# Six of ten PSUM banks kept across the down stage, and the acts-times-gates product moved from VectorE to GpSimd

## The chip, the cores and the metric

The kernel runs on one core of one Trainium2 chip. The metric is the device time of one execution in microseconds (us), the median of three runs. Engines are named as in the profile: PE is TensorE, DVE is VectorE, ACT is ScalarE, POOL is GpSimd, SP is SyncE, which here only issues transfers.

## The reference

One trunk layer on 1024 tokens of width 1024: a gated recurrence and an attention, then PEER, a retrieval over 128 x 128 = 16384 single-neuron experts, and a last norm. The change touches only the second half of PEER:

```
experts = (e1 * PEER_NKEYS + e2).reshape(t, hk)      # 128 experts per token
gates = jax.nn.softmax(top_s, axis=-1).reshape(t, hk)
pre = einsum('td,tkd->tk', xb, u_tab[eb])            # "up"
act = gelu(pre) * gb
y   = einsum('tk,tkd->td', act, v_tab[eb])           # "down"
```

All is float32.

## The kernel before

**Two ways to the same sum.** The first three tiles of 128 tokens (F = 3) are computed by rows: each token's 128 expert rows are fetched by number and added with a weight. The other five tiles (640 tokens) are computed densely: the activation of every expert is multiplied by a gate, zero where the expert wasn't picked, and the down stage multiplies this 640 x 16384 matrix by the whole table v. Both ways run side by side in `experts_down` (L1562), which is the stage of this case.

**The dense way.** The 128 keys x go in NG = 32 groups of C = 4. For each key, SP loads a piece of v (512 KB, ring of 3), the activations (320 KB, ring of 4, the tile `acts_times_gates`), and for each group the gates (1280 KB). `multiply(x)` (L1650) puts acts times gates in place. To multiply float32 on TensorE, every operand is split in a rounded high part and the rest: ACT writes `v_hi` (L1642) and, once the product is there, `w_hi` (L1644). DVE writes the rests: `low_of_v(x)` (L1666, tile `v_lo`) and `low(x)` (L1658, tile `w_lo`). TensorE then makes, for a group, BANKS = 10 sums (five token tiles, two halves of 512 columns): j = 0 to 9, each of 4 keys x 3 products = 12 matmuls. A sum lands in one of the 8 PSUM banks in turn, and DVE adds it to `y` (`add(n, j)`, L1672), which frees the bank. TensorE's group n+1 may start only when all four `low` and `low_of_v` of that group are done (L1714, L1715). The four parts are double buffered by group.

**The row way.** GpSimd issues `fetch(k)` (L1616), an indirect transfer of one row per partition (512 KB) into a ring of 5, and DVE adds it with its weight (`add_row(k)`, L1680). There are 3 x 128 = 384. Fetch k waits until row k-5 has been added (L1619).

**The order on DVE** is written out by hand (L1698 to L1709). Group n has ten steps j. In step j DVE runs, if they are due, multiply and low_of_v of a key of the next group (j = 0, 2, 5, 7) or low of that key (j = 1, 3, 6, 8), then the rows whose turn it is (364 rows over 320 steps, so 11.375 a group), and then `add(n, j)`. The order on GpSimd (L1623 to L1631) sets how many fetches are issued before the transfer queue goes on to the next key:

```
asked = lambda x: min(max(FIRST_ROWS + ROW_RING + (x - C) * (AXPYS - FIRST_ROWS) // NK, FIRST_ROWS), AXPYS)
```

that is, 25 + floor((x - 4) * 2.84375) fetches come ahead of key x.

Of the kernel before, what the change touches and what calls it, by code (L numbers as in the profile page):

```python
# [4 lines left out]
ALU = mybir.AluOpType  # L5
ACT = mybir.ActivationFunctionType
AX_X = mybir.AxisListType.X
F32 = mybir.dt.float32
# [4 lines left out]
P = 128  # L13
HALF = 512
# [1173 lines left out]
def experts_up(nc, d, m, sem):  # L1188
# [15 lines left out]
    DOTS = F * P  # L1204
    RING = 6
    QUARTERS = 4 * NK
# [27 lines left out]
    with ExitStack() as own_memory:  # L1234
# [14 lines left out]
        gate_hi, gate_lo = sb("gateT_hi", [P, 2, P], F32R), sb("gateT_lo", [P, 2, P])  # L1249
        rows = sb("u_rows", [P, RING, D])  # L1250
        dots = m.row_weight
# [14 lines left out]
        key_step, route_turned, routeT_done = sem("key_step"), sem("route_turned"), sem("routeT_done")  # L1266
        rows_known, fetched = sem("rows_known"), [sem(f"u_row_in{b}") for b in range(RING)]
        dot_done, dots_read, weighted = sem("dot_done"), sem("dots_read"), sem("row_weights_done")
# [12 lines left out]
        with nc.Block() as block:  # L1281
# [127 lines left out]
            def _(pool):  # L1409
# [7 lines left out]
                def fetch(k):  # L1417
                    f, slot = divmod(k, P)
                    if slot == 0:
                        pool.wait_ge(rows_known, f + 1)  # L1420
                    if k >= RING:
                        pool.wait_ge(dot_done, k - RING + 1)
                    pool.indirect_dma_start(rows[:, k % RING], None, d.peer_u, bass.IndirectOffsetOnAxis(  # L1423
                        ap=m.row_of[:, f, slot:slot + 1], axis=0)).then_inc(fetched[k % RING], 16)
# [137 lines left out]
def experts_down(nc, d, m, sem):  # L1562
# [5 lines left out]
    NT, F = S // P, m.ROWS_TILES  # L1568
    DENSE = S - F * P
    C, PART = 4, 32  # L1570
    NG = NK // C
    BANKS = (NT - F) * D // HALF
    RING = 8
    V_RING, W_RING, ROW_RING = 3, 4, 5
    AXPYS = F * P
    FIRST_ROWS = 20
# [1 line left out]
    with ExitStack() as own_memory:  # L1578
        sb = lambda n, s, t=F32: own_memory.enter_context(nc.sbuf_tensor(n, s, t))
        prod = sb("acts_times_gates", [P, W_RING, DENSE])  # L1580
        gate = sb("gates_group", [P, 2, DENSE // PART, C, PART])
# [1 line left out]
        whi, wlo = sb("w_hi", [P, 2, C, DENSE], F32R), sb("w_lo", [P, 2, C, DENSE], F32R)  # L1583
        vhi, vlo = sb("v_hi", [P, 2, C, D], F32R), sb("v_lo", [P, 2, C, D], F32R)
        rows = sb("v_rows", [P, ROW_RING, D])
        out = own_memory.enter_context(nc.psum_tensor("expert_out", [P, RING, HALF], F32))

        y_in, y_rest_in = sem("x2_in"), sem("x2_rest_in")
        a_in = [sem(f"acts_in{b}") for b in range(W_RING)]
        g_in = [sem(f"gates_in{b}") for b in range(2)]  # L1590
        v_in = [sem(f"v_in{b}") for b in range(V_RING)]
        prod_done, whi_done, wlo_done = sem("prod_done"), sem("w_hi_done"), sem("w_lo_done")
        vhi_done, vlo_done = sem("v_hi_done"), sem("v_lo_done")
        out_done, out_read = sem("expert_out_done"), sem("expert_out_read")
        fetched, row_added = [sem(f"v_row_in{b}") for b in range(ROW_RING)], sem("v_row_added")

        with nc.Block() as block:
            @block.sync
# [15 lines left out]
            @block.gpsimd  # L1614
            def _(pool):
                def fetch(k):  # L1616
                    slot, f = divmod(k, F)
                    if k >= ROW_RING:
                        pool.wait_ge(row_added, k - ROW_RING + 1)  # L1619
                    pool.indirect_dma_start(rows[:, k % ROW_RING], None, d.peer_v, bass.IndirectOffsetOnAxis(  # L1620
                        ap=m.row_of[:, f, slot:slot + 1], axis=0)).then_inc(fetched[k % ROW_RING], 16)

                asked = lambda x: min(max(FIRST_ROWS + ROW_RING + (x - C) * (AXPYS - FIRST_ROWS) // NK, FIRST_ROWS), AXPYS)  # L1623
                for k in range(asked(0)):
                    fetch(k)
                for x in range(NK):
                    pool.wait_ge(vhi_done, x + 1)
                    for k in range(asked(x), asked(x + 1)):
                        fetch(k)
                for k in range(asked(NK), AXPYS):  # L1630
                    fetch(k)  # L1631
# [14 lines left out]
            @block.vector  # L1646
            def _(dve):
                v = nc.vector

                def multiply(x):  # L1650
                    n, c = divmod(x, C)
                    dve.wait_ge(a_in[x % W_RING], 16 * (x // W_RING + 1))
                    if c == 0:
                        dve.wait_ge(g_in[n % 2], 16 * (n // 2 + 1))
                    tokens = prod[:, x % W_RING].rearrange("p (t k) -> p t k", k=PART)
                    v.tensor_tensor(tokens, tokens, gate[:, n % 2, :, c, :], ALU.mult).then_inc(prod_done, 1)  # L1656

                def low(x):  # L1658
                    n, c = divmod(x, C)
                    dve.wait_ge(whi_done, x + 1)  # L1660
                    if c == 0 and n >= 2:
                        dve.wait_ge(out_done, BANKS * (n - 1))
                    v.tensor_tensor(wlo[:, n % 2, c], prod[:, x % W_RING], whi[:, n % 2, c].bitcast(F32), ALU.subtract  # L1663
                                    ).then_inc(wlo_done, 1)

                def low_of_v(x):  # L1666
                    n, c = divmod(x, C)
                    dve.wait_ge(vhi_done, x + 1)
                    v.tensor_tensor(vlo[:, n % 2, c], vt[:, x % V_RING], vhi[:, n % 2, c].bitcast(F32), ALU.subtract
                                    ).then_inc(vlo_done, 1)  # L1670

                def add(n, j):  # L1672
                    t, half = divmod(j, 2)
                    bank = BANKS * n + j
                    dve.wait_ge(out_done, bank + 1)
                    cols = slice(half * HALF, (half + 1) * HALF)
                    v.tensor_tensor(m.y[:, F + t, cols], m.y[:, F + t, cols], out[:, bank % RING], ALU.add  # L1677
                                    ).then_inc(out_read, 1)

                def add_row(k):  # L1680
                    slot, f = divmod(k, F)
                    dve.wait_ge(fetched[k % ROW_RING], 16 * (k // ROW_RING + 1))
                    if k >= F:
                        dve.wait_ge(row_added, k - F + 1)
                    v.scalar_tensor_tensor(out=m.y[:, f], in0=rows[:, k % ROW_RING],  # L1685
                                           scalar=m.row_weight[:, f, slot:slot + 1], in1=m.y[:, f],
                                           op0=ALU.mult, op1=ALU.add).then_inc(row_added, 1)

                dve.wait_ge(y_in, 16)
                for k in range(FIRST_ROWS):  # L1690
                    add_row(k)
                for x in range(C):
                    low_of_v(x)
                    multiply(x)
                    low(x)
                dve.wait_ge(y_rest_in, 16)
                added = lambda s: FIRST_ROWS + s * (AXPYS - FIRST_ROWS) // (NG * BANKS)
                for n in range(NG):  # L1698
                    for j in range(BANKS):
                        for x in range(C):  # L1700
                            if n + 1 < NG and j == x * BANKS // C:
                                multiply(C * (n + 1) + x)
                            if n + 1 < NG and j == x * BANKS // C + 1:
                                low(C * (n + 1) + x)
                            if n + 1 < NG and j == x * BANKS // C + (0 if BANKS < 3 * C else 2):
                                low_of_v(C * (n + 1) + x)
                        for k in range(added(BANKS * n + j), added(BANKS * n + j + 1)):
                            add_row(k)
                        add(n, j)  # L1709

            @block.tensor
            def _(pe):
                for n in range(NG):
                    pe.wait_ge(wlo_done, C * (n + 1))  # L1714
                    pe.wait_ge(vlo_done, C * (n + 1))  # L1715
                    for j in range(BANKS):
                        t, half = divmod(j, 2)
                        bank = BANKS * n + j
                        tokens, cols = slice(t * P, (t + 1) * P), slice(half * HALF, (half + 1) * HALF)
                        if bank >= RING:  # L1720
                            pe.wait_ge(out_read, bank - RING + 1)
                        terms = [(a, e, c) for c in range(C) for a, e in ((whi, vhi), (whi, vlo), (wlo, vhi))]
                        for k, (a, e, c) in enumerate(terms):
                            last = nc.tensor.matmul(out[:, bank % RING], a[:, n % 2, c, tokens], e[:, n % 2, c, cols],  # L1724
                                                    start=k == 0, stop=k == len(terms) - 1)
                        last.then_inc(out_done, 1)


# [185 lines left out]
```

## Time and profile before

| | |
|---|---|
| median of 3 runs | 3281.61 us (3280.7 to 3283.81) |
| profiled execution | 3266.46 us, span 3264.7 us |
| DVE, PE, POOL, ACT busy | 2415.6, 2913.1, 1339.1, 1211.5 us |
| down stage, first row added to last sum added | 2220.16 to 3240.61 us |
| one group of it | 30.75 us |

Busy time over the whole span mixes several stages; the argument needs only the down stage, so the rows below are read with a window. A DVE row's duration overlaps the next one's start by some 0.08 us; what an instruction costs in a full queue is the distance between two starts.

### The profile page before, as it was taken

The page shows a single profiled execution, that of the slowest core. Times are in us where ns is not written, and L with a number is a line of the kernel's source. Part 1 is how long each engine was busy: PE and PEld are TensorE (multiplying, and loading weights), DVE is VectorE, ACT ScalarE, POOL GpSimd, SP SyncE. Part 2 cuts the span into 40 slices and gives each one's busy share as a digit, 9 for nine tenths or more (in the row PEclk, how much of TensorE's full clock was granted, in tenths as well). Part 3 has the DMA queues.
Part 4 walks back from the last instruction along what each step waited for, and adds up shares of the span by engine and source line. Part 5 has one row for each costly group of instructions (what it writes and reads, how often), then busy time and mean ns, then how long its engine had stood idle before and what let it go on. Part 6 is the DMA issues. An engine that isn't in the chain of part 4 may idle for free. (4 is left out here: it accounts for less than half of the span.)

```text
span 3264.7 us, 40188 instructions
## 1 busy us (share of the span) xinstructions
PE 2913.1 (89%) x15015; PEld 2398.5 (73%) x15015; DVE 2415.6 (74%) x4285; ACT 1211.5 (37%) x2462; POOL 1339.1 (41%) x1095
## 2 busy tenths in 40 slices
PE   7998998988798889999999999991999999999996
PEld 3345545543798888999999999991777777777775
DVE  1073353622397699979788988875999999999997
ACT  2112223211111225777778778751222222222221
POOL 1030000000287457555545555543444464454455
PEclk9988899899899999999999999995999999999998
DMA  5000001011210248998989999988999999999996
GB/s 152 1 20 20 0 1 52 0 58 45 65 34 27 93 163 298 335 352 321 351 324 375 345 325 357 357 333 327 360 356 351 361 348 355 355 350 344 356 357 219
DMA packets 309203, 754.28 MB, mean 231 GB/s; under 512 B 22848, under 2 KB 133440, under 8 KB 306448
## 3 DMA queue, kind: packets, MB, share of 16 engines
q0 software_dynamic: 111104, 403.02, 33.7%
q1 hardware_dynamic: 196848, 344.50, 30.0%
q10 hardware_dynamic: 1056, 4.19, 0.3%
q8 instruction: 119, 1.95, 0.2%
q14 instruction: 76, 0.62, 0.1%
HBM read 659.35 MB, written 92.27 MB: 230 GB/s over the span
## 5 line engine op out<-in xcount | busy, mean ns | idle before, releaser
L1620 POOL DMA_INDIRECT v_rows<-in_peer_v,row_numbers x384 | 523.9, 1364 | 524.3 <-DVE y L1685 432.5
L1325 PE MATMUL expert_pre<-h2T,uT_hi 128*128 128x320 f32 x4096 | 679.8, 315 | 58.7 <-DVE uT_lo L1510 31.7
L1423 POOL DMA_INDIRECT u_rows<-in_peer_u,row_numbers x384 | 539.5, 1405 | 434.6 <-DVE row_weights L1527 377.7
L1325 PEld LDWEIGHTS expert_pre<-h2T,uT_hi 128*128 128x128 f32 x4096 | 621.5, 192 | 64.0 <-DVE uT_lo L1510 35.3
L1724 PE MATMUL expert_out<-v_hi,w_hi 128*128 128x512 f32 x1280 | 510.5, 399 | 133.5 <-DVE w_lo L1663 133.5
L1685 DVE SCALAR_TENSOR_TENSOR y<-v_rows,row_weights,y 128x1024 f32<-128x1024 f32 x384 | 487.0, 1277 | 40.9 <-DMA v_rows<-in_peer_v,row_numbers 23.9
L1724 PE MATMUL expert_out<-v_lo,w_hi 128*128 128x512 f32 x1280 | 506.1, 395 | 0.0
L1724 PE MATMUL expert_out<-v_hi,w_lo 128*128 128x512 f32 x1280 | 505.9, 395 | 0.0
L1527 DVE CUSTOM_DVE_ANT_0 u_rows<-u_rows,h_rows_kept 128x1024 f32<-128x1024 f32 x384 | 469.2, 1249 | 5.3 <-DMA u_rows<-in_peer_u,row_numbers 5.3
L1724 PEld LDWEIGHTS expert_out<-v_hi,w_hi 128*128 128x128 f32 x1280 | 245.5, 192 | 197.1 <-DVE w_lo L1663 146.0
L1644 ACT ACTIVATE w_hi<-acts_times_gates 128x640 fp32r<-128x640 f32 x128 | 94.8, 741 | 735.6 <-DVE acts_times_gates L1656 610.3
L1325 PE MATMUL expert_pre<-h2T,uT_lo 128*128 128x320 f32 x2048 | 343.0, 308 | 0.0
L1325 PEld LDWEIGHTS expert_pre<-h2T,uT_lo 128*128 128x128 f32 x2048 | 312.7, 188 | 0.0
L1724 PEld LDWEIGHTS expert_out<-v_hi,w_lo 128*128 128x128 f32 x1280 | 244.8, 191 | 52.3
L1724 PEld LDWEIGHTS expert_out<-v_lo,w_hi 128*128 128x128 f32 x1280 | 245.6, 192 | 50.9
L1510 DVE TENSOR_TENSOR uT_lo<-u_chunk,uT_hi 128x1024 fp32r<-128x1024 f32 x104 | 127.2, 1223 | 139.0 <-ACT uT_hi L1361 129.2
L1383 ACT ACTIVATE second_hot_lo<-second_hot_hi,gateT_lo 128x128 fp32r<-128x128 f32 x640 | 203.2, 392 | 64.3 <-DVE second_hot_hi L1521 62.0
L1677 DVE TENSOR_TENSOR y<-y,expert_out 128x512 f32<-128x512 f32 x320 | 217.1, 678 | 2.6 <-PE expert_out L1724 2.4
L1386 ACT ACTIVATE second_hot_hi<-second_hot_hi,gateT_hi 128x128 fp32r<-128x128 f32 x640 | 203.5, 392 | 0.0
L1368 ACT ACTIVATE pick_memory<-spread_ps 128x512 f32<-128x512 f32 x160 | 179.6, 1122 | 21.4 <-PE spread_ps L1317 19.5
L1092 POOL CAST wq_hi<-wq_tile 128x1024 fp32r<-128x1024 f32 x16 | 16.6, 1039 | 407.0 <-DMA wq_tile<-in_peer_wq 360.6
L1375 ACT ACTIVATE expert_acts<-expert_pre 128x320 f32<-128x320 f32 x256 | 112.4, 440 | 185.4 <-PE expert_pre L1325 183.7
(264 smaller groups left out, 4324.5 us busy)
## 6 DMA issues: line engine op xcount, KB each, us to landing
u_chunk<-in_peer_u_turned SPq DMA_DIRECT2D x128, 512.0 KB
v_chunk<-in_peer_v SPq DMA_DIRECT2D x128, 512.0 KB
acts_dram<-expert_acts SPq DMA_DIRECT2D x128, 320.0 KB
gates_dram<-pick_memory SPq DMA_DIRECT2D x20, 2048.0 KB
acts_times_gates<-acts_dram SPq DMA_DIRECT2D x128, 320.0 KB
gates_group<-gates_dram SPq DMA_DIRECT2D x32, 1280.0 KB
wq_tile<-in_peer_wq SPq DMA_DIRECT2D x16, 512.0 KB, 3.9
w_qkv<-in_w_in SPq DMA_DIRECT2D x12, 512.0 KB, 7.1
```

Of the source, the lines that this page charges most:

```text
L1325: last = nc.tensor.matmul(pre[:, (2 * c + half) % 4, 0:WIDTH], part[:, c % 2, k], m.h2T[:, t, k, HALVES[half]], start=n == 0, stop=n == le ...
L1368: A(spread[:, part % 2, :, col * GROUP:(col + 1) * GROUP].rearrange("p e t -> p t e"), spread_ps[:, g % 2], ACT.Copy).then_inc(spread_read, 1)
L1375: A(act_out[:, c % 2, half * WIDTH:(half + 1) * WIDTH], pre[:, (2 * c + half) % 4, 0:WIDTH], ACT.Gelu_apprx_tanh).then_inc(act_done, 1)
L1383: A(second_lo[:, g % SLOTS, j], second_hi[:, g % SLOTS, j].bitcast(F32), ACT.Identity, scale=gate_lo[:, t % 2, first + j:first + j + 1])
L1386: last = A(second_hi[:, g % SLOTS, j], second_hi[:, g % SLOTS, j].bitcast(F32), ACT.Identity, scale=gate_hi[:, t % 2, first + j:first + j ...
L1423: pool.indirect_dma_start(rows[:, k % RING], None, d.peer_u, bass.IndirectOffsetOnAxis(ap=m.row_of[:, f, slot:slot + 1], axis=0)).then_inc ...
L1510: v.tensor_tensor(ulo[:, c % 2], u[:, c % 2], uhi[:, c % 2].bitcast(F32), ALU.subtract).then_inc(ulo_dve, 1)
L1527: v.tensor_tensor_reduce(out=rows[:, k % RING], in0=rows[:, k % RING], in1=m.h2_kept[:, f], scale=1.0, scalar=0.0, op0=ALU.mult, op1=ALU.a ...
L1620: pool.indirect_dma_start(rows[:, k % ROW_RING], None, d.peer_v, bass.IndirectOffsetOnAxis(ap=m.row_of[:, f, slot:slot + 1], axis=0)).then ...
L1677: v.tensor_tensor(m.y[:, F + t, cols], m.y[:, F + t, cols], out[:, bank % RING], ALU.add).then_inc(out_read, 1)
L1685: v.scalar_tensor_tensor(out=m.y[:, f], in0=rows[:, k % ROW_RING], scalar=m.row_weight[:, f, slot:slot + 1], in1=m.y[:, f], op0=ALU.mult, ...
L1724: last = nc.tensor.matmul(out[:, bank % RING], a[:, n % 2, c, tokens], e[:, n % 2, c, cols], start=k == 0, stop=k == len(terms) - 1)
```

## The change

Six of the ten sums (j = 1, 2, 4, 6, 7, 9) get a PSUM bank for themselves and are accumulated in it over all 32 groups; DVE adds them to `y` once, in the last group. The other four (`TURNING`: 0, 3, 5, 8) share the two banks that are left and are added in every group, as before. `multiply` leaves DVE and stands in GpSimd's program, ahead of the fetches of the same key. Everything else, the order of low, low_of_v and the rows among it, stays where it was.

```
-    RING = 8
+    TURNING = [0, 3, 5, 8]
+    KEPT = [j for j in range(BANKS) if j not in TURNING]
+    RING = 8 - len(KEPT)
...
+        def place(n, j):
+            if j in KEPT:
+                i = KEPT.index(j)
+                return i // 2, i % 2, i
+            i = TURNING.index(j)
+            return (len(KEPT) + i) // 2, i % 2, len(KEPT) + (len(TURNING) * n + i) % RING
...
+                def multiply(x):
+                    n, c = divmod(x, C)
+                    pool.wait_ge(a_in[x % W_RING], 16 * (x // W_RING + 1))
+                    if c == 0:
+                        pool.wait_ge(g_in[n % 2], 16 * (n // 2 + 1))
+                    tokens = prod[:, x % W_RING].rearrange("p (t k) -> p t k", k=PART)
+                    pool.tensor_tensor(tokens, tokens, gate[:, n % 2, :, c, :], ALU.mult).then_inc(prod_done, 1)
...
                 for x in range(NK):
+                    multiply(x)
                     pool.wait_ge(vhi_done, x + 1)
                     for k in range(asked(x), asked(x + 1)):
                         fetch(k)
...
                 for x in range(C):
                     low_of_v(x)
-                    multiply(x)
                     low(x)
...
-                            if n + 1 < NG and j == x * BANKS // C:
-                                multiply(C * (n + 1) + x)
...
-                        add(n, j)
+                        if j in TURNING or n == NG - 1:
+                            add(n, j)
...
-                        if bank >= RING:
-                            pe.wait_ge(out_read, bank - RING + 1)
+                        turn = len(TURNING) * n + TURNING.index(j) if j in TURNING else 0
+                        if turn >= RING:
+                            pe.wait_ge(out_read, turn - RING + 1)
+                        opens = j in TURNING or n == 0
+                        closes = j in TURNING or n == NG - 1
...
-                                                    start=k == 0, stop=k == len(terms) - 1)
+                                                    start=opens and k == 0, stop=closes and k == len(terms) - 1)
```

DVE's queue before, in one half of a group of the down stage (steps 0 to 3, or 5 to 8, which read alike). `acts_times_gates` is written by multiply, `v_lo` by low_of_v, `w_lo` by low; `y` from `v_rows` is a row, `y` from `expert_out` is an add.

```order
L1656 TENSOR_TENSOR acts_times_gates<-acts_times_gates,gates_group 128x640
L1669 TENSOR_TENSOR v_lo<-v_chunk,v_hi 128x1024
L1685 SCALAR_TENSOR_TENSOR y<-v_rows,row_weights,y 128x1024
L1677 TENSOR_TENSOR y<-y,expert_out 128x512
L1663 TENSOR_TENSOR w_lo<-acts_times_gates,w_hi 128x640
L1685 SCALAR_TENSOR_TENSOR y<-v_rows,row_weights,y 128x1024
L1677 TENSOR_TENSOR y<-y,expert_out 128x512
L1656 TENSOR_TENSOR acts_times_gates<-acts_times_gates,gates_group 128x640
L1669 TENSOR_TENSOR v_lo<-v_chunk,v_hi 128x1024
L1685 SCALAR_TENSOR_TENSOR y<-v_rows,row_weights,y 128x1024
L1677 TENSOR_TENSOR y<-y,expert_out 128x512
L1663 TENSOR_TENSOR w_lo<-acts_times_gates,w_hi 128x640
```

The same steps on DVE in the changed kernel, up to the end of step 8 (or 3):

```order
L1680 TENSOR_TENSOR v_lo<-v_chunk,v_hi 128x1024
L1695 SCALAR_TENSOR_TENSOR y<-v_rows,row_weights,y 128x1024
L1687 TENSOR_TENSOR y<-y,expert_out 128x512
L1674 TENSOR_TENSOR w_lo<-acts_times_gates,w_hi 128x640
L1695 SCALAR_TENSOR_TENSOR y<-v_rows,row_weights,y 128x1024
L1680 TENSOR_TENSOR v_lo<-v_chunk,v_hi 128x1024
L1695 SCALAR_TENSOR_TENSOR y<-v_rows,row_weights,y 128x1024
L1674 TENSOR_TENSOR w_lo<-acts_times_gates,w_hi 128x640
L1695 SCALAR_TENSOR_TENSOR y<-v_rows,row_weights,y 128x1024
L1687 TENSOR_TENSOR y<-y,expert_out 128x512
```

The multiplies are gone, and the adds of the kept banks with them; low stands at the same step, now behind fewer instructions.

GpSimd's queue in the down stage before is 384 fetches with nothing between them. In the changed kernel it reads, with the semaphores that each instruction waits for (`v_row_added` counts the rows that DVE has added, `acts_in` and `gates_in` are landed transfers):

```order
L1639 TENSOR_TENSOR acts_times_gates<-acts_times_gates,gates_group 128x640 [waits acts_in2]
L1630 DMA v_rows<-in_peer_v,row_numbers 128x1024 [waits v_row_added,v_hi_done]
L1630 DMA v_rows<-in_peer_v,row_numbers 128x1024 [waits v_row_added] x2
L1639 TENSOR_TENSOR acts_times_gates<-acts_times_gates,gates_group 128x640 [waits acts_in3]
L1630 DMA v_rows<-in_peer_v,row_numbers 128x1024 [waits v_row_added,v_hi_done]
L1630 DMA v_rows<-in_peer_v,row_numbers 128x1024 [waits v_row_added] x2
```

Each multiply now stands behind two or three fetches, and the engine takes its queue in order.

## Rows read from the trace of the kernel before

**Rows 1.** Busy time per engine in the steady part of the down stage.
```profile
core 0: us, PE busy (x) PEld busy (x) DVE busy (x) ACT busy (x) POOL busy (x), PEclk, DMA share, GB/s
2300.00:3200.00 900.00, 838.71 (x3581) 683.17 (x3580) 891.77 (x992) 203.04 (x237) 464.14 (x337) 0.98 0.99 352
```

**Rows 2.** Waits, same stretch: who, for whom, total us, times, longest us.
```profile
POOL v_rows L1620 <- DVE y L1685: 393.8, 240, 4.7
...
PE expert_out L1724 <- DVE w_lo L1663: 61.3, 28, 4.3
...
DVE y L1685 <- DMA v_rows<-in_peer_v,row_numbers: 7.3, 5, 2.6
```

**Rows 3.** Groups of instructions, DVE, 2220 to 3241 us: busy, mean ns, idle before.
```profile
L1685 DVE SCALAR_TENSOR_TENSOR y<-v_rows,row_weights,y 128x1024 f32<-128x1024 f32 x384 | 487.0, 1277 | 40.9 <-DMA v_rows<-in_peer_v,row_numbers 23.9 <-DMA y<-x_dram 16.8
L1677 DVE TENSOR_TENSOR y<-y,expert_out 128x512 f32<-128x512 f32 x320 | 217.1, 678 | 2.6 <-PE expert_out L1724 2.4
...
L1663 DVE TENSOR_TENSOR w_lo<-acts_times_gates,w_hi 128x640 fp32r<-128x640 f32 x128 | 104.5, 816 | 3.2 <-ACT w_hi L1644 3.2
L1656 DVE TENSOR_TENSOR acts_times_gates<-acts_times_gates,gates_group 128x640 f32<-128x640 f32 x128 | 104.5, 816 | 1.8 <-DMA gates_group<-gates_dram 1.8
```

**Rows 4.** Timeline of DVE within one group: start, duration, instruction.
```profile
2598.52 0.82 DVE L1656 TENSOR_TENSOR acts_times_gates<-acts_times_gates,gates_group 128x640 f32<-128x640 f32 x1
2599.26 1.22 DVE L1669 TENSOR_TENSOR v_lo<-v_chunk,v_hi 128x1024 fp32r<-128x1024 f32 x1
2600.39 1.28 DVE L1685 SCALAR_TENSOR_TENSOR y<-v_rows,row_weights,y 128x1024 f32<-128x1024 f32 x1
2601.59 0.68 DVE L1677 TENSOR_TENSOR y<-y,expert_out 128x512 f32<-128x512 f32 x1
2602.18 0.82 DVE L1663 TENSOR_TENSOR w_lo<-acts_times_gates,w_hi 128x640 fp32r<-128x640 f32 x1
2602.92 1.28 DVE L1685 SCALAR_TENSOR_TENSOR y<-v_rows,row_weights,y 128x1024 f32<-128x1024 f32 x1
...
2608.44 1.22 DVE L1669 TENSOR_TENSOR v_lo<-v_chunk,v_hi 128x1024 fp32r<-128x1024 f32 x1
```

**Rows 5.** Timeline of POOL beside them, and one fetch later on.
```profile
2601.94 0.94 POOL L1620 DMA_INDIRECT v_rows<-in_peer_v,row_numbers  x1 [2.73 <-DVE y L1685]
...
2608.36 2.12 POOL L1620 DMA_INDIRECT v_rows<-in_peer_v,row_numbers  x1 [0.30 <-issue]
...
2659.43 3.37 POOL L1620 DMA_INDIRECT v_rows<-in_peer_v,row_numbers  x1 [0.31 <-issue]
```

**Rows 6.** Timeline of ACT beside them.
```profile
2608.55 0.74 ACT L1644 ACTIVATE w_hi<-acts_times_gates 128x640 fp32r<-128x640 f32 x1 [6.47 <-DVE acts_times_gates L1656]
```

**Rows 7.** Timeline of PE at the ends of two groups.
```profile
3178.95 0.39 PE L1724 MATMUL expert_out<-v_hi,w_lo 128*128 128x512 f32 x1
3181.36 0.50 PE L1724 MATMUL expert_out<-v_hi,w_hi 128*128 128x512 f32 x1 [2.02 <-DVE w_lo L1663]
...
3208.48 0.39 PE L1724 MATMUL expert_out<-v_hi,w_lo 128*128 128x512 f32 x1
3212.11 0.50 PE L1724 MATMUL expert_out<-v_hi,w_hi 128*128 128x512 f32 x1 [3.25 <-DVE w_lo L1663]
```

**Rows 8.** GpSimd's float32 tensor_tensor elsewhere: count, min/median/max ns of each.
```profile
L1414 POOL TENSOR_TENSOR uT_lo<-u_chunk,uT_hi x24: 2352/2408/3958, 1085.5 to 1277.2; 128x1024 fp32r<-128x1024 f32 x24
...
L1003 POOL TENSOR_TENSOR decode<-decode x6: 456/461/463, 923.4 to 1117.3; 128x128 f32<-128x128 f32 x6
```

**Rows 9.** Timeline, DVE and POOL, where both ran a two-input instruction.
```profile
1181.64 2.28 DVE L1474 TENSOR_TENSOR pick_memory<-pair_digits,iota 128x2048 f32<-128x2048 bf16 x1
...
1183.96 4.37 DVE L1479 TENSOR_TENSOR pick_memory<-pick_memory,top_indices_f 128x2048 f32<-128x2048 f32 x1
...
1182.50 3.68 POOL L1414 TENSOR_TENSOR uT_lo<-u_chunk,uT_hi 128x1024 fp32r<-128x1024 f32 x1 [4.64 <-ACT uT_hi L1361]
...
1201.00 2.29 DVE L1479 TENSOR_TENSOR pick_memory<-pick_memory,top_indices_f 128x2048 f32<-128x2048 f32 x1
```

More of the change, by code:

```diff
@@ L1585, in experts_down @@
         rows = sb("v_rows", [P, ROW_RING, D])
-        out = own_memory.enter_context(nc.psum_tensor("expert_out", [P, RING, HALF], F32))
+        out = own_memory.enter_context(nc.psum_tensor("expert_out", [P, 8, HALF], F32))
         y_in, y_rest_in = sem("x2_in"), sem("x2_rest_in")
@@ L1593, in experts_down @@
         vhi_done, vlo_done = sem("v_hi_done"), sem("v_lo_done")
-        out_done, out_read = sem("expert_out_done"), sem("expert_out_read")
+        out_done, out_read, kept_read = sem("expert_out_done"), sem("expert_out_read"), sem("kept_out_read")
         fetched, row_added = [sem(f"v_row_in{b}") for b in range(ROW_RING)], sem("v_row_added")
+        def place(n, j):
[4 more added lines that the diff above has]
+            return (len(KEPT) + i) // 2, i % 2, len(KEPT) + (len(TURNING) * n + i) % RING
         with nc.Block() as block:
@@ L1648, in _ @@
                 v = nc.vector
[L1650 to L1656, printed above, removed]
                 def low(x):
@@ L1672, in add @@
                 def add(n, j):
-                    t, half = divmod(j, 2)
-                    bank = BANKS * n + j
-                    dve.wait_ge(out_done, bank + 1)
+                    t, half, bank = place(n, j)
+                    dve.wait_ge(out_done, BANKS * n + j + 1)
                     cols = slice(half * HALF, (half + 1) * HALF)
-                    v.tensor_tensor(m.y[:, F + t, cols], m.y[:, F + t, cols], out[:, bank % RING], ALU.add
-                                    ).then_inc(out_read, 1)
+                    v.tensor_tensor(m.y[:, F + t, cols], m.y[:, F + t, cols], out[:, bank], ALU.add
+                                    ).then_inc(out_read if j in TURNING else kept_read, 1)
                 def add_row(k):
@@ L1716, in _ @@
                     for j in range(BANKS):
-                        t, half = divmod(j, 2)
-                        bank = BANKS * n + j
+                        t, half, bank = place(n, j)
                         tokens, cols = slice(t * P, (t + 1) * P), slice(half * HALF, (half + 1) * HALF)
-                        if bank >= RING:
-                            pe.wait_ge(out_read, bank - RING + 1)
+                        turn = len(TURNING) * n + TURNING.index(j) if j in TURNING else 0
[3 more added lines that the diff above has]
+                        closes = j in TURNING or n == NG - 1
                         terms = [(a, e, c) for c in range(C) for a, e in ((whi, vhi), (whi, vlo), (wlo, vhi))]
                         for k, (a, e, c) in enumerate(terms):
-                            last = nc.tensor.matmul(out[:, bank % RING], a[:, n % 2, c, tokens], e[:, n % 2, c, cols],
-                                                    start=k == 0, stop=k == len(terms) - 1)
+                            last = nc.tensor.matmul(out[:, bank], a[:, n % 2, c, tokens], e[:, n % 2, c, cols],
+                                                    start=opens and k == 0, stop=closes and k == len(terms) - 1)
                         last.then_inc(out_done, 1)
```

## The prediction

> **What bounds the kernel now.** First I read the busy times of the steady part of the down stage [rows 1]. Of 900 us DVE is busy 892, PE 839, and the DMA engines have a share of 0.99; three things are close to their end together, and DVE is the closest. Then the waits [rows 2]: PE waited 61.3 us in 28 pieces, all of them for DVE's `w_lo`, the last thing a group needs before it may start. DVE waited 7.3 us for rows and for nothing else of size. GpSimd waited 393.8 us for DVE's row adds: it is idle, but it is idle because each of its fetches has to wait for a row. Last, the timelines. A group of 120 matmuls starts at 3181.36 and the next at 3212.11, so a group takes 30.75 us; its own matmuls run from 3181.36 to 3208.48 plus one step, 27.2 us [rows 7]. So PE could go 3.5 us a group faster, if DVE let it.
>
> DVE's prices are the distances between two starts [rows 4]: multiply 0.74 us, low_of_v 1.13, a row 1.20, an add 0.60, low 0.74. A group on DVE is 11.375 rows, 10 adds and 4 of each of the others: 13.65 + 6.0 + 10.44 = 30.1 us, against 30.75 measured.
>
> **What the change removes.** All 128 multiplies [rows 3] at 0.74 us: 95 us. The adds of six banks in 31 of 32 groups, 186 of 320, at 0.60 us: 112 us. Together 206 us of DVE's queue, 6.6 us a group, which leaves DVE 23.5 us of work for each group, less than PE's 27.2. A reader who stops here forecasts a gain that ends at PE.
>
> **What it adds: a wait in a circle.** GpSimd's multiply(x) stands behind all fetches before it, and with f = floor((x-4) x 2.84375) the last of these is the (25+f)th, which by the ring of five may start only when DVE has added its (20+f)th row. Call that the releasing row. Written out from L1697 to L1709, DVE comes to exactly this row just ahead of its own low(x), and low(x) needs the product. So for each key DVE adds the releasing row, GpSimd then fetches, then multiplies, ACT then writes `w_hi`, and only then can DVE go on with low(x). No buffer softens this: the ring of five rows is what ties the fetch to the row. Before, the product came from DVE itself, a step ahead.
>
> What DVE has to do between the releasing row and low(x) I counted from the code for x = 4 to 127: (A) low_of_v, row, add, 53 times; (A2) the same with two rows, 8 times; (B) low_of_v, row, 28 times; (C) nothing, 27 times; (D) one row, 7 times. One more, x = 4, has a long list and no stall.
>
> The chain, with time 0 where DVE's next instruction would start:
> - The fetch starts 0.35 us later (2601.94 against 2601.59) and takes 0.94 us when DVE is in an add [rows 4, 5]; I take the same when DVE is idle. It ends at 1.29.
> - When DVE is in low_of_v, the fetch waits for it: the one at 2608.36 ends at 2610.48, which is 0.82 us after low_of_v's end at 2609.66 [rows 4, 5]. So in A, A2 and B it ends at 1.22 + 0.82 = 2.04, in D at 1.28 + 0.82 = 2.10.
> - The multiply of 128x640 on GpSimd is not in the trace. Its float32 tensor_tensor takes 2.41 us for 1024 elements and 0.46 for 128 [rows 8], so 2.18 ns an element more, and 0.46 + 512 x 0.00218 = 1.57 us, if runs of 32 elements cost nothing extra. Lower end: 1.2 us, half of 2.41; in proportion to the elements it would be 1.5, and no row shows GpSimd faster than that. Upper end: the 2.41 us of 1024 elements.
> - ACT's `w_hi` starts 0.03 us after the product and takes 0.74 (2608.55; DVE's multiply before it began 0.74 us before low_of_v at 2608.44 and so ended at 2608.52) [rows 4, 6]; 0.02 more to low.
>
> So in C low starts at 1.29 + 1.57 + 0.79 = 3.65, a stall of 3.65 us. In D: 2.10 + 1.57 + 0.79 - 1.20 = 3.26.
>
> For A and B it matters what happens when both engines read two operands. The multiply of 1024 elements at 1182.50 took 3.68 us: it stood until DVE's instruction ended at 1183.92 and ran 2.26 us from there. DVE's next one, started at 1183.96, took 4.37 us instead of the 2.29 it takes alone [rows 9]: 2.08 us lost. Whoever comes second stands until the first is done. So in A and B the multiply, ready at 2.04, starts when the row ends at 2.41, and runs 1.57 - 0.15 = 1.42 us to 3.83; low can start at 4.62. DVE is there at 2.33 in B, a stall of 2.29, and at 2.93 in A, a stall of 1.69. In A2 the second row is held for 2.08 - 0.84 = 1.24 us and nothing else stalls.
>
> The Trainium skill states this as a rule on its page "SBUF — State Buffer", section "SBUF: two separate sides": the port pair that VectorE and GpSimd share is an exclusive lock held for the whole instruction, and a VectorE instruction with two SBUF inputs collides with a GpSimd one that reads SBUF. This case's trace agrees, with the 2.08 us above [rows 9].
>
> Sum: A 53 x 1.69 = 89.6; A2 8 x 1.24 = 9.9; B 28 x 2.29 = 64.1; C 27 x 3.65 = 98.6; D 7 x 3.26 = 22.8; together 285 us. A fetch sometimes misses the first gap on DVE and ends only after the next instruction, as the one at 2659.43 with 3.37 us [rows 5]; for the 81 windows with low_of_v and a row after it (A and B) I take one in five, an estimate, at 0.97 us each (fetch end 2.41 + 0.82 = 3.23 instead of 2.04, so multiply from there instead of from 2.41): 16 us. Against it stand 206 us of work removed, DVE's 7.3 us of waits for rows, which a slower stage no longer has [rows 2], and 3.2 us of waits for ACT at the first four keys [rows 3], whose products GpSimd now makes during the first twenty rows. 285 + 16 - 206 - 10 = 84 us more. That is 2.7 us a group, 33.5 instead of 30.75.
>
> **What else the change touches.** The wait of PE for a bank falls away for six banks; rows 2 have no such wait, so it was worth nothing, and costs nothing. PE's work is the same. A group of 33.5 us leaves PE 6 us idle instead of 3.5; its granted clock in the steady part was 0.98 [rows 1], and it may fall by a fifth before 27.2 us become 33.5, so I cost that at nothing. Transfers become fewer per us, so no price there. The kept sums are added once at the end, in the same ten adds of the last group as before, one behind each bank.
>
> **The times.** Profiled execution: 3266.46 + 84 = 3350 us. The median of the runs is 3281.61, 15 us above the profiled execution; I carry the difference over: 3281.6 + 84 = 3366 us.
>
> **Rivals.**
> - *The work removed is gained, PE or the transfers end it.* 31 groups x 3.5 us = 110 us, 3172 us. It needs GpSimd to be a key ahead of DVE. For it: GpSimd is busy only 464 of 900 us. Against it: its idle time is exactly the wait for rows [rows 2], and the fetches stand ahead of the multiply in the queue. 3%.
> - *Only the held port costs.* If the products came early enough, each of 124 multiplies would hold DVE 1.24 us: 154 - 206 = 52 us less, 3230 us. As mechanism of this kernel it needs the same lead of GpSimd, or a fetch that hands over to the next instruction before its 0.94 us are done. 5%. It is the rule of the Trainium skill's page “SBUF — State Buffer” taken as the whole price; the trace bears out the lock [rows 9], and not that it is the whole.
> - *The circle is there, but short.* Multiply of 1.2 us, no missed gaps: every stall 0.37 us less, 239 - 206 - 10 = 23 us more, 3305 us. About break-even within 0.2% needs another 20 us off, which would be a fetch that costs the chain less than 0.8 us. Near this end 14%, of which 4% lie within no change.
> - *The product is slow on GpSimd.* In the gates tile and in the product the 640 elements come in twenty runs of 32. With 2.41 us, every stall is 0.84 us longer: 388 + 16 - 206 - 10 = 188 us more, 3470 us. Nothing in the trace shows such an access on GpSimd. 15%.
>
> **How the numbers follow.** Forecast 63%, with its own range 3325 to 3415 (multiply 1.35 to 1.9 us); the rest as above. The range reaches from the short circle to near the slow product: 3305 to 3455 us. A measurement of this kernel tells 0.2%, some 6.6 us, from no change. Faster: 8%. Within 0.2%: 4%. Slower: 88%.
>
> **What would show it.** In the changed kernel's profile DVE waits for ACT's `w_hi` at low, about 115 times and some 290 us in all, where before it was 3.2 us. DVE's busy time in the steady stretch falls from 99% to near 72%. POOL's multiply takes about 1.6 us, up to 1.2 us more where it stood behind DVE. A matmul group starts every 33 to 34 us, and PE waits for `w_lo` 5 to 7 us each time. In windows without work (C) the stall is 3.6 us. The row adds that follow a multiply in A2 last 2.5 us instead of 1.28. Wrong would be: multiplies that start before the releasing row is added, a DVE without stalls at low, or matmul groups at 27 to 30 us.

## The result: 2.9% slower, and the profile after

The changed kernel takes 3371.77 us (median of 4 runs, 3367.62 to 3378.04) against 3281.15 before; the ratio is 1.0287, interval 1.0253 to 1.0320. Forecast was 3366 us, range 3305 to 3455. The profiled execution is the slowest of the four: 3378.04 us, span 3376.2, so between the two profiled executions lie 112 us. In a second set of runs the changed kernel took 3375.14 us against 3270.72, 104 us more; the ratio was 1.0329 (1.0306 to 1.0352).

First the steady stretch, in the columns of [rows 1]:

```profile
2300.00:3200.00 900.00, 783.77 (x3219) 635.79 (x3218) 637.50 (x625) 180.60 (x214) 579.60 (x412) 0.93 0.92 319
```

DVE, busy 892 of 900 us before, is busy 638. PE, for whose sake one would free DVE, fell from 839 to 784. Work was taken off the fullest engine, and every engine but POOL now does less per microsecond. The waits of the same stretch, in the columns of [rows 2], say why:

```profile
ACT w_hi L1663 <- POOL acts_times_gates L1639: 721.5, 107, 10.2
POOL v_rows L1630 <- DVE y L1695: 285.8, 167, 6.2
DVE w_lo L1674 <- ACT w_hi L1663: 261.8, 107, 3.9
...
PE expert_out L1734 <- DVE w_lo L1674: 116.2, 27, 7.2
```

Read them as a circle: ACT waits for POOL, POOL for DVE, DVE for ACT. The third row is new. PE's wait for `w_lo` was 61.3 us and is 116.2.

The groups of DVE and POOL over the down stage (busy, mean ns, idle before), which answer to [rows 3]:

```profile
L1695 DVE SCALAR_TENSOR_TENSOR y<-v_rows,row_weights,y 128x1024 f32<-128x1024 f32 x384 | 490.9, 1288 | 31.3 <-DMA y<-x_dram 16.8 <-DMA v_rows<-in_peer_v,row_numbers 14.4
L1680 DVE TENSOR_TENSOR v_lo<-v_chunk,v_hi 128x1024 fp32r<-128x1024 f32 x128 | 156.9, 1226 | 1.9 <-ACT v_hi L1661 1.9
L1674 DVE TENSOR_TENSOR w_lo<-acts_times_gates,w_hi 128x640 fp32r<-128x640 f32 x128 | 105.6, 825 | 301.6 <-ACT w_hi L1663 301.6
L1687 DVE TENSOR_TENSOR y<-y,expert_out 128x512 f32<-128x512 f32 x134 | 91.1, 680 | 10.5 <-PE expert_out L1734 10.4
```
```profile
L1639 POOL TENSOR_TENSOR acts_times_gates<-acts_times_gates,gates_group 128x640 f32<-128x640 f32 x128 | 217.5, 1700 | 7.8 <-DMA acts_times_gates<-acts_dram 4.2 <-DMA gates_group<-gates_dram 1.3
```

DVE waits 301.6 us at low, where it waited 3.2. The 186 adds and 128 multiplies are gone. The rows last almost as long as before (1288 against 1277 ns).

One turn of the circle in the timeline. DVE:

```profile
2908.12 0.82 DVE L1674 TENSOR_TENSOR w_lo<-acts_times_gates,w_hi 128x640 fp32r<-128x640 f32 x1 [1.64 <-ACT w_hi L1663]
2908.86 1.28 DVE L1695 SCALAR_TENSOR_TENSOR y<-v_rows,row_weights,y 128x1024 f32<-128x1024 f32 x1
2910.05 1.22 DVE L1680 TENSOR_TENSOR v_lo<-v_chunk,v_hi 128x1024 fp32r<-128x1024 f32 x1
2911.19 1.28 DVE L1695 SCALAR_TENSOR_TENSOR y<-v_rows,row_weights,y 128x1024 f32<-128x1024 f32 x1
2916.04 0.82 DVE L1674 TENSOR_TENSOR w_lo<-acts_times_gates,w_hi 128x640 fp32r<-128x640 f32 x1 [3.58 <-ACT w_hi L1663]
...
2918.58 2.47 DVE L1695 SCALAR_TENSOR_TENSOR y<-v_rows,row_weights,y 128x1024 f32<-128x1024 f32 x2
2920.97 1.22 DVE L1680 TENSOR_TENSOR v_lo<-v_chunk,v_hi 128x1024 fp32r<-128x1024 f32 x1
2922.10 1.28 DVE L1695 SCALAR_TENSOR_TENSOR y<-v_rows,row_weights,y 128x1024 f32<-128x1024 f32 x1
2923.30 0.68 DVE L1687 TENSOR_TENSOR y<-y,expert_out 128x512 f32<-128x512 f32 x1
2926.64 0.83 DVE L1674 TENSOR_TENSOR w_lo<-acts_times_gates,w_hi 128x640 fp32r<-128x640 f32 x1 [2.66 <-ACT w_hi L1663]
...
2933.22 0.82 DVE L1674 TENSOR_TENSOR w_lo<-acts_times_gates,w_hi 128x640 fp32r<-128x640 f32 x1 [2.23 <-ACT w_hi L1663]
```

POOL and ACT beside it:

```profile
2912.74 0.93 POOL L1630 DMA_INDIRECT v_rows<-in_peer_v,row_numbers  x1 [0.65 <-DVE y L1695]
2913.68 1.56 POOL L1639 TENSOR_TENSOR acts_times_gates<-acts_times_gates,gates_group 128x640 f32<-128x640 f32 x1
...
2921.01 1.99 POOL L1630 DMA_INDIRECT v_rows<-in_peer_v,row_numbers  x1 [0.30 <-issue]
2923.30 0.94 POOL L1630 DMA_INDIRECT v_rows<-in_peer_v,row_numbers  x1 [0.30 <-issue]
2924.26 1.57 POOL L1639 TENSOR_TENSOR acts_times_gates<-acts_times_gates,gates_group 128x640 f32<-128x640 f32 x1
```
```profile
2915.27 0.74 ACT L1663 ACTIVATE w_hi<-acts_times_gates 128x640 fp32r<-128x640 f32 x1 [6.24 <-POOL acts_times_gates L1639]
```

The releasing row, which starts at 2911.19, ends at 2912.47; fetch from 2912.74, multiply from 2913.68, `w_hi` from 2915.27, low at 2916.04. That is window C, 3.58 us of stall where 3.65 was worked out.

### The profile page after: what moved, and what is told of

Same layout as the page of the kernel before. It is cut to its first block and busy times, and to the rows that moved or that the text cites. A ratio compares the mean times of both kernels' runs of the same rounds, so it can differ in the third digit from the quotient of the medians.

```text
span 3376.2 us, 40004 instructions
## 1 busy us (share of the span) xinstructions
PE 2956.9 (88%) x15015; PEld 2431.1 (72%) x15015; DVE 2224.4 (66%) x3971; ACT 1208.4 (36%) x2462; POOL 1531.3 (45%) x1223
## 5 line engine op out<-in xcount | busy, mean ns | idle before, releaser
L1734 PE MATMUL expert_out<-v_hi,w_hi 128*128 128x512 f32 x1280 | 527.3, 412 | 201.5 <-DVE w_lo L1674 201.5
L1630 POOL DMA_INDIRECT v_rows<-in_peer_v,row_numbers x384 | 500.1, 1302 | 426.1 <-DVE y L1695 358.0
L1734 PE MATMUL expert_out<-v_lo,w_hi 128*128 128x512 f32 x1280 | 520.8, 407 | 0.0
L1734 PE MATMUL expert_out<-v_hi,w_lo 128*128 128x512 f32 x1280 | 519.1, 406 | 0.0
L1695 DVE SCALAR_TENSOR_TENSOR y<-v_rows,row_weights,y 128x1024 f32<-128x1024 f32 x384 | 490.9, 1288 | 31.3 <-DMA y<-x_dram 16.8
L1734 PEld LDWEIGHTS expert_out<-v_hi,w_hi 128*128 128x128 f32 x1280 | 255.2, 199 | 269.1 <-DVE w_lo L1674 214.9
L1674 DVE TENSOR_TENSOR w_lo<-acts_times_gates,w_hi 128x640 fp32r<-128x640 f32 x128 | 105.6, 825 | 301.6 <-ACT w_hi L1663 301.6
L1734 PEld LDWEIGHTS expert_out<-v_hi,w_lo 128*128 128x128 f32 x1280 | 253.9, 198 | 55.9
L1734 PEld LDWEIGHTS expert_out<-v_lo,w_hi 128*128 128x128 f32 x1280 | 255.1, 199 | 53.8
L1639 POOL TENSOR_TENSOR acts_times_gates<-acts_times_gates,gates_group 128x640 f32<-128x640 f32 x128 | 217.5, 1700 | 7.8 <-DMA acts_times_gates<-acts_dram 4.2
L1368 ACT ACTIVATE pick_memory<-spread_ps 128x512 f32<-128x512 f32 x160 | 179.6, 1122 | 22.1 <-PE spread_ps L1317 21.8
```

Of the source, the lines that this page charges most:

```text
L1368: A(spread[:, part % 2, :, col * GROUP:(col + 1) * GROUP].rearrange("p e t -> p t e"), spread_ps[:, g % 2], ACT.Copy).then_inc(spread_read, 1)
L1639: pool.tensor_tensor(tokens, tokens, gate[:, n % 2, :, c, :], ALU.mult).then_inc(prod_done, 1)
L1734: last = nc.tensor.matmul(out[:, bank], a[:, n % 2, c, tokens], e[:, n % 2, c, cols], start=opens and k == 0, stop=closes and k == len(ter ...
```

## The experiments

Ratios are to the kernel before on the same chip, since its own median differed from one set of runs to another (3281.2 with the result, then 3267.8, 3270.7 and 3274.2 us). The theory: the product is a link of a circle that runs through GpSimd's queue. Its rivals: GpSimd is simply the slower place for it, or the kept sums cost something.

**Each part alone: kept_only.** Against the changed kernel:

```
-                    multiply(x)            # GpSimd
                     pool.wait_ge(vhi_done, x + 1)
...
                     low_of_v(x)
+                    multiply(x)            # VectorE, as before
                     low(x)
...
+                            if n + 1 < NG and j == x * BANKS // C:
+                                multiply(C * (n + 1) + x)
```
 

> Only the first part of the change: six sums stay in PSUM, VectorE keeps the multiply. Theory (circle through GpSimd's queue): nothing waits on GpSimd, VectorE has 26.5 us of work a group, less than the 27.2 us of the matmuls; a group takes 27.5 to 28.5 us, the whole 3190 to 3215 us, and low waits under 20 us in all. Rival 1 (the kept sums themselves cost something, such as matmuls that accumulate across groups running slower): slower than 3270 us and the matmul's mean above before's 395 to 399 ns. Rival 2 (transfers were already the bound, share 0.99): no gain, 3265 to 3285 us.

Measured: 3202.02 us, ratio 0.9803 (0.9780 to 0.9826). So the kept sums are a gain of 2% alone, 66 us. The steady stretch, first before, then kept_only (columns as in [rows 1]):

```profile
2300.00:3100.00 800.00, 743.96 (x3173) 605.87 (x3172) 791.77 (x881) 180.73 (x211) 401.66 (x300) 0.97 0.99 353
```
```profile
2300.00:3100.00 800.00, 785.16 (x3424) 644.64 (x3423) 756.37 (x779) 196.37 (x227) 525.05 (x324) 0.99 1.03 380
```

PE is busy 785 of 800 us: with only the adds taken off DVE, PE is near its end, as the first rival of the prediction has it. Low waited 3.2 us, and from its first to its last, 2261.8 to 3143.4, a group takes 28.4 us, as the theory said. Rival 1 of the expectation falls (the matmuls' mean is 393 to 391 ns, before 399 to 395), and so does rival 2: the transfers moved 380 GB/s, above the 353 that went with a share of 0.99. So the share of 0.99 before was not yet a bound.

**Each part alone: mult_only.**

```
-    TURNING = [0, 3, 5, 8]
+    TURNING = list(range(BANKS))      # all ten sums turn over 8 banks
```

> Only the second part: GpSimd multiplies, all ten sums turn over the eight banks and are added in every group. Theory (circle): low's stalls in the windows with little work stay near 3 us each; adds lengthen VectorE's part and shorten the stalls, so the whole stays close to the changed kernel, 3370 to 3410 us, and the six kept sums are worth under 40 us here though they are worth some 75 us alone. Rival (the two parts add up independently): the changed kernel is 91 us slower than before and kept_only some 75 us faster, so mult_only would be 3281 + 91 + 75 = 3447 us or more.

Measured: 3404.05 us, ratio 1.0421 (1.0397 to 1.0446), a time inside what the theory said. The rival's 3447 us was reckoned from the other set's 3281; by ratios the sum of the parts is 1.0287 + 0.0197 = 1.0484, and the measured one is 0.6% below it (1.0% with the second set's 1.0329), so the parts do share something, though less than 3447 makes it look. The kept sums are worth 2% alone, and beside the moved multiply 1.3% (1.0421 against 1.0287) or 0.9% (against 1.0329). That is 44 or 30 us, so whether it is under the 40 us that was expected is not settled. On DVE:

```profile
L1695 DVE SCALAR_TENSOR_TENSOR y<-v_rows,row_weights,y 128x1024 f32<-128x1024 f32 x384 | 571.3, 1498 | 31.3 <-DMA y<-x_dram 16.9 <-DMA v_rows<-in_peer_v,row_numbers 14.4
...
L1674 DVE TENSOR_TENSOR w_lo<-acts_times_gates,w_hi 128x640 fp32r<-128x640 f32 x128 | 104.8, 818 | 148.0 <-ACT w_hi L1663 148.0
```

With more adds to do, DVE stalls half as long at low (148 us for 302), but now the multiply meets rows: their mean is 1498 ns instead of the 1277 of the kernel before, 85 us over 384 rows. The 95 us of multiplies taken off DVE are less than these 148 + 85.

**Ahead of the fetches: lead1.**

```
+                multiply(0)
                 for x in range(NK):
-                    multiply(x)
+                    if x + 1 < NK:
+                        multiply(x + 1)
                     pool.wait_ge(vhi_done, x + 1)
```

> The changed kernel with one edit: GpSimd multiplies key x+1 ahead of the fetches of key x, so a product no longer stands behind the fetch that waits for the releasing row. Theory (circle): low's 302 us of waits fall below 30 us, and what is left is the held port, at most 124 times 1.24 us: 3281 - 206 - 10 + 154 = 3220 us (3190 to 3240). Rival (GpSimd is simply the slower place for this product, by its 1.7 us or by the shared port): the multiplies cost the same wherever they stand, 3350 us or more.

Measured: 3259.64 us, ratio 0.9967 (0.9950 to 0.9983). The multiply is on the same engine and no shorter (1844 ns in the mean, 1700 in the changed kernel); to stand ahead of one key's two or three fetches and not behind them is worth 3.2%. Low waits 1.6 us. "The slower place" falls, and the circle stands. But the time lies outside the expected 3190 to 3240 us. The 3220 us was 40 us short, and 53 short if it is reckoned from this set's 3267.8:

```profile
L1697 DVE SCALAR_TENSOR_TENSOR y<-v_rows,row_weights,y 128x1024 f32<-128x1024 f32 x384 | 555.2, 1452 | 101.2 <-DMA v_rows<-in_peer_v,row_numbers 83.9 <-DMA y<-x_dram 16.6
L1682 DVE TENSOR_TENSOR v_lo<-v_chunk,v_hi 128x1024 fp32r<-128x1024 f32 x128 | 160.9, 1257 | 4.9 <-ACT v_hi L1663 4.9
L1676 DVE TENSOR_TENSOR w_lo<-acts_times_gates,w_hi 128x640 fp32r<-128x640 f32 x128 | 154.5, 1207 | 1.6 <-ACT w_hi L1665 1.6
```
```profile
L1639 POOL TENSOR_TENSOR acts_times_gates<-acts_times_gates,gates_group 128x640 f32<-128x640 f32 x128 | 236.0, 1844 | 67.4 <-DMA gates_group<-gates_dram 54.1 <-DMA acts_times_gates<-acts_dram 11.4
```

The held port, DVE's instructions standing while GpSimd multiplies, costs 67 us on the rows (175 ns x 384), 50 on low and 5 on low_of_v against their durations before: 122 us, below the 154 allowed for. The rest is a new wait: the multiply of a group's first key, now a key earlier, waits for its gates (54.1 us), the fetches stand behind it, and DVE waits 83.9 us for rows, 60 more than before. With 206 us removed, 122 + 60 leave a gain of 24 us; the profiled executions differ by 18.

**lead1_ring6**: lead1 with `ROW_RING` 6 in place of 5. 

> lead1 with a ring of six rows. In lead1 GpSimd waited 54 us for gates, with the row fetches queued behind it, and VectorE then 84 us for rows. If that is why lead1 gained 40 us less than expected, one more row in the ring covers it: VectorE waits under 35 us for rows and the ratio to before is 0.975 to 0.988. If instead the held port alone makes up the difference, the ratio stays 0.995 to 0.999 and the row adds last longer.

Measured: 3236.56 us, ratio 0.9907 (0.9889 to 0.9925), between the two expectations. DVE waited 38.4 us for rows, 45 less than in lead1 and just over the 35 that were expected; part of that came back as held port (rows 1538 ns, low_of_v 1394, low 1034: 100 + 23 + 28 = 151 us, the 154 that the prediction's rival of the held port alone had). DVE is busy 775 of 800 us again (731 in lead1), so fewer multiplies fall where DVE is idle anyway.

**One row earlier: ring6 and one_fetch_later.** Two ways to let the multiply stand one fetch earlier, one with a deeper ring, one without:

```
ring6:            ROW_RING = 6;  asked = ... FIRST_ROWS + ROW_RING - 1 + ...
one_fetch_later:  ROW_RING = 5;  asked = ... FIRST_ROWS + ROW_RING - 1 + ...
```

> The changed kernel with a ring of six rows in place of five, while as many fetches as before stand ahead of each multiply: the releasing row is one row earlier, nothing else moves. Theory (circle): low's stalls shrink by up to one row, 1.2 us, each; in windows A and B the held port of 1.24 us takes their place, so low waits 90 to 150 us in all and the whole is 3240 to 3300 us. Rival (a multiply costs what it costs on GpSimd, the row ring has no part in it): 3370 us as the changed kernel.

> The changed kernel with one number changed in the order: one fetch less stands ahead of each multiply, with the ring of five rows as it was. Theory (circle through the order of the queue): the releasing row is one earlier, as with a ring of six, so it does the same as ring6, a ratio to before of 0.99 to 1.01. Rival (ring6 gained by its deeper ring, rows arriving earlier): as the changed kernel, 1.02 or more.

Measured: ring6 3254.92 us, ratio 0.9969 (0.9952 to 0.9986), low waits 91.0 us; one_fetch_later 3280.83 us, ratio 1.0025 (1.0009 to 1.0041), low waits 94.3. One number in the order takes back nine tenths of the loss (from 1.0329 in the same set), 94 us. It doesn't do so by ending the cost of the product, but by exchanging it. Against after_again low waits 211 us less, while the rows last 185 ns longer in the mean and low_of_v 222, 71 + 28 us of held port, and DVE waits 20 us more for rows: 92 us less in all. Of one_fetch_later:

```profile
L1695 DVE SCALAR_TENSOR_TENSOR y<-v_rows,row_weights,y 128x1024 f32<-128x1024 f32 x384 | 562.8, 1475 | 52.1 <-DMA v_rows<-in_peer_v,row_numbers 35.2 <-DMA y<-x_dram 16.7
L1680 DVE TENSOR_TENSOR v_lo<-v_chunk,v_hi 128x1024 fp32r<-128x1024 f32 x128 | 184.5, 1441 | 1.5 <-ACT v_hi L1661 1.5
L1674 DVE TENSOR_TENSOR w_lo<-acts_times_gates,w_hi 128x640 fp32r<-128x640 f32 x128 | 104.6, 817 | 94.3 <-ACT w_hi L1663 94.3
```

The ring's depth is not what did most of it; it adds half a per cent, and that shows in DVE's waits for rows, 17.6 us with six rows and 35.2 with five.

**The length of the product: half_product.** This kernel leaves half of the tokens' activations without their gates.

```
-  tokens = prod[:, x % W_RING].rearrange("p (t k) -> p t k", k=PART)
-  pool.tensor_tensor(tokens, tokens, gate[:, n % 2, :, c, :], ALU.mult)
+  tokens = prod[:, x % W_RING].rearrange("p (t k) -> p t k", k=PART)[:, 0:DENSE // PART // 2]
+  pool.tensor_tensor(tokens, tokens, gate[:, n % 2, 0:DENSE // PART // 2, c, :], ALU.mult)
```

> The changed kernel, but GpSimd multiplies only the first ten of twenty runs of 32 (the other tokens' activations are left without their gates); everything else is as it was. By 2.18 ns an element the product takes 0.7 us less. Theory (each product is a link of the chain before low): some 115 stalls shrink by 0.7 us each, 75 to 90 us less than the changed kernel of the same call; low's waits fall from 302 us to some 215. Rival (the time goes to handing over between engines or to the queue's order, not to the product's length): within 15 us of the changed kernel.

Measured: 3289.01 us against 3375.14 of the changed kernel in the same set (after_again, below): 86 us less for a multiply that is 0.69 us shorter by its mean (1014 against 1701 ns). Waits at low, of half_product and then of after_again (who, for whom, total, times, longest):

```profile
DVE w_lo L1674 <- ACT w_hi L1663: 216.8, 124, 3.2
```
```profile
DVE w_lo L1674 <- ACT w_hi L1663: 305.1, 125, 4.0
```

88 us less wait, 86 us less time, 0.7 us for each of some 125 waits: the product stands whole on the path.

**after_again**: 

> The changed kernel itself, so that half_product and one_fetch_later have it on the same chip: a ratio to before of 1.025 to 1.032, as in its first runs.

Measured: 3375.14 us, ratio 1.0329 (1.0306 to 1.0352), just over the expected interval.

**Can kept_only be bettered? kept_ring6 and kept_again.** 

> kept_only with a ring of six rows. kept_only had PE busy 785 of 800 us and VectorE waiting 44 us for rows. If the matmuls bound it, VectorE's waits fall and the time doesn't: within 6 us of kept_only. If late rows bound it, it is 15 us or more faster.

> kept_only again, on the same chip as kept_ring6: a ratio to before of 0.978 to 0.983, as in its first runs.

Measured: kept_again 3206.53 us, ratio 0.9788 (0.9761 to 0.9815); kept_ring6 3216.12 us, ratio 0.9820 (0.9792 to 0.9848), 10 us slower by the medians, which neither expectation has. The intervals of the two ratios overlap, but both hold the spread of the same kernel before; the runs themselves, 3204.8 to 3207.5 and 3215.1 to 3219.8 us, don't. DVE's waits for rows fell from 46.9 to 16.8 us and its waits for gates rose from 21.8 to 55.3:

```profile
L1666 DVE TENSOR_TENSOR acts_times_gates<-acts_times_gates,gates_group 128x640 f32<-128x640 f32 x128 | 105.0, 821 | 22.7 <-DMA gates_group<-gates_dram 21.8 <-issue 0.3
```
```profile
L1666 DVE TENSOR_TENSOR acts_times_gates<-acts_times_gates,gates_group 128x640 f32<-128x640 f32 x128 | 105.2, 822 | 55.3 <-DMA gates_group<-gates_dram 55.3
```

The first is kept_again, the second kept_ring6. That a sixth row in flight takes time from the gates' transfer fits, but was not tried apart; what bounds kept_only in its last per cent stays open. kept_only is the best version found: 2% faster than before and, by the two ratios, 5% faster than the changed kernel.

## Why the prediction was right

By its own steps, with the prediction's number first:

- *Work removed.* 206 us of DVE's queue. DVE's busy time fell by 191 us (2415.6 to 2224.4). The 5 us of held instructions below, and the 0.08 us by which two neighbours overlap, lost at each of 124 stalls (10 us), make it 206.
- *The circle and its windows.* 285 + 16 us, of which 10 was meant as held rows, so 291 us of waits at low. Measured 301.6. The forecast counts a stall from where DVE's next instruction would start, the profile from where the last one ends, 0.08 us later, so 0.08 us has to be added to each measured stall before the two are compared. C 3.65 us: 3.58 at 2916.04. B 2.29: 2.23 at 2933.22. A 1.69: 1.64 at 2908.12. The table has all windows, in us:

| window | times | forecast | waits in the profile | the same + 0.08 each |
|---|---|---|---|---|
| A (with missed gaps) | 53 | 89.6 + 16 | 106.4 | 110.6 |
| A2 | 8 | 9.9 | 13.1 | 13.7 |
| B | 28 | 64.1 | 62.0 | 64.2 |
| C | 27 | 98.6 | 96.9 | 99.1 |
| D | 7 | 22.8 | 22.4 | 23.0 |
| x = 4 | 1 | 0 | 1.0 | 1.1 |

- *The missed gaps.* The longer A at 2926.64, 2.66 us, has the size that I gave a missed gap, but another reason: after two rows in a row (2918.58) the last fetch but one (2921.01, 1.99 us) was still under way, and the last one, 2923.30, came late. So it was in all 19 long windows of A, and in none of B. The 16 us stood for something that happens, under the wrong name; that its size came out near (110.6 for 105.6 us) is in part luck.
- *A2 came out differently.* The forecast had its second row held, 2.5 us long, and no stall. No row of these eight windows was held; low stalled 1.64 us in each, because the last fetch ended only in the second row and the multiply, at 2451.84, stood behind that one:

```profile
2449.74 2.48 DVE L1695 SCALAR_TENSOR_TENSOR y<-v_rows,row_weights,y 128x1024 f32<-128x1024 f32 x2
...
2454.44 0.83 DVE L1674 TENSOR_TENSOR w_lo<-acts_times_gates,w_hi 128x640 fp32r<-128x640 f32 x1 [1.63 <-ACT w_hi L1663]
```
```profile
2449.84 1.99 POOL L1630 DMA_INDIRECT v_rows<-in_peer_v,row_numbers  x1 [0.31 <-issue]
2451.84 1.80 POOL L1639 TENSOR_TENSOR acts_times_gates<-acts_times_gates,gates_group 128x640 f32<-128x640 f32 x1
```

  So the count of stalls was off as well: 115 forecast, 124 measured, the eight of A2 and the one of x = 4 more.
- *The multiply.* 1.57 us from a line through two other shapes. Measured 1.56 where DVE was idle, 1.70 in the mean; the runs of 32 cost nothing, so the rival of a slow product falls.
- *The held port.* 10 us forecast; rows 11 ns and low_of_v 10 ns longer in the mean, 4 + 1 us. The 4 us are three rows beside the products of the first keys, near 2262, ahead of the circle; in it the port held next to nothing. The rows of the other kernels show what the lock costs beside a full DVE: 122 us in lead1 and 151 in lead1_ring6, where products come early. In the changed kernel it is small because here it is GpSimd's multiply that comes second and stands until DVE's instruction ends, or DVE is already waiting. The Trainium skill's page "SBUF — State Buffer", section "SBUF: two separate sides", calls this lock exclusive. This row of lead1 agrees, a low of 0.82 us that met a multiply of GpSimd (2820.46, 1.72 us):

```profile
2820.68 2.18 DVE L1676 TENSOR_TENSOR w_lo<-acts_times_gates,w_hi 128x640 fp32r<-128x640 f32 x1
```

  Whoever had taken the rule as the whole price would have forecast 3230 us.
- *Waits given back.* 10 us forecast. DVE's waits for rows fell by 9.5 us (23.9 to 14.4), the ACT waits of the first four keys went, and 8 us came up that I had at nothing: waits of add for PE rose from 2.4 to 10.4 us, 7 of them after the last low, when the kept sums are added one behind the other.
- *The sum.* For the profiled executions I had 84 us. From the first low to the last, 2262.8 to 3211.3 before and 2270.6 to 3320.4 after, it is 948.5 and 1049.8 us, 101 more. In this stretch DVE idles 12 us before and 307 after, 295 more, and works 193 us less, so the sum closes. Of the 17 us above the forecast 11 are stalls (311.7 for 301.0 in the table); the other waits gave back 5 us here and not 10; and low_of_v and low last a little longer. Before the first low the changed kernel lost 8 us and behind the last 2, which makes the 112. Medians: 84 forecast, 91 measured in the first set and 104 in the second. That 3366 us came within 6 us of 3371.77 is in part luck: the kernel before had its highest median, 3281, in the very set in which the forecast was measured.
- *PE.* A group of 33.5 us: 1049.8 / 31 = 33.9. Its waits for `w_lo` were forecast at 5 to 7 us a group and are 4.3 in the mean (116.2 in 27). PE was busy 87% of the stretch, 29.5 us a group and not 27.2, at a granted clock of 0.93 instead of 0.98.
- *Rivals.* The gain that ends at PE is real, but belongs to kept_only: it came as soon as nothing waited on GpSimd. Its price was too high, though: 3.5 us a group was read from two groups at the end, while PE's waits are 2.2 us in the mean (61.3 in 28, [rows 2]), and kept_only gained 66 us and not 110. "Only the held port" needs the product early, and lead1 and ring6 show both the mechanism and what it takes. The slow product didn't come.

The shortest form of the proof is the pair half_product and one_fetch_later: 0.7 us less in the link gives 0.7 us a key, and one fetch less ahead of it takes nine tenths of the loss away.

What the first reading of the profile got half wrong: DMA at a share of 0.99 counted as "close to its end". kept_only moved 380 GB/s where 353 had gone with 0.99.

## What to carry to other kernels

Before you move an instruction to an idle engine, write down what that engine waits for in its queue and whether the waiter and the releaser then form a circle: here POOL was idle 436 of 900 us, 394 of them waiting for DVE's rows, and that idle time could not be spent on something that DVE needs at once. If it must stand there, put it ahead of the waits and not behind them; that was worth 3%. Even there, held instructions and new waits took nearly all of the gain: lead1 is 0.3% faster than before. And try the parts of a change alone: this one was a gain of 2% joined to a loss of 4%.

## What the runs showed of the hardware

TensorE's granted clock fell at the start of many groups of the changed kernel. After a wait of 2.65 us for `w_lo`, at 2916.92, the first matmuls took 0.63 to 0.79 us; at the end of the group 0.39. The stretches from there (columns as in [rows 1]):

```profile
2916.92:2919.50 2.58, 2.58 (x6) 2.10 (x7) 2.58 (x3) 0.04 (x1) 0.67 (x1) 0.50 0.69 275
2919.50:2922.00 2.50, 2.50 (x10) 1.97 (x10) 2.50 (x3) 0.00 (x0) 2.19 (x2) 0.85 0.34 68
2922.00:2930.00 8.00, 8.00 (x37) 6.62 (x36) 5.34 (x7) 1.69 (x2) 5.55 (x5) 1.00 0.90 322
```

0.50 is the lower of its two levels, 1.2 GHz, and 1.00 the upper, 2.4 GHz. In the steady stretch (2300 to 3200 us) 18 of 27 groups that followed a wait began with a first matmul of 0.71 to 0.80 us and not 0.50. The kernel before had this too, in 6 of 28. The length of the wait alone doesn't tell which group it is. The kernel before has a slow start after 3.26 us and a fast one after 3.25 (3212.11, [rows 7]), and the changed kernel has a fast one after 4.25:

```profile
2633.81 0.80 PE L1724 MATMUL expert_out<-v_hi,w_hi 128*128 128x512 f32 x1 [3.26 <-DVE w_lo L1663]
```
```profile
2410.90 0.50 PE L1734 MATMUL expert_out<-v_hi,w_hi 128*128 128x512 f32 x1 [4.25 <-DVE w_lo L1674]
```

In the changed kernel this costs next to nothing in the steady stretch: DVE, which sets the pace there, waited 0.6 us in 900 for PE's sums. What such starts cost a kernel bound by PE, no run here shows.

An indirect fetch on GpSimd is also held by DVE's two-input instructions: a fetch that takes 0.93 us beside an idle DVE (2912.74) took 1.99 at 2921.01, beside low_of_v and a row; it ended 0.81 us after low_of_v did. The multiply, that fetch and DVE's rows all take turns in these traces, so an idle share of POOL beside a full DVE says little of how fast work there will go.
